# Final mLSTM states of a hybrid decoder step: keys as the stationary operand, states turned back later, stored from the used queries' place

## The reference, cut to what matters

```python
w_state = jnp.exp(b[..., -1:] - b + ig - m_new[..., None])
C_new = decay[..., None, None] * C + jnp.einsum('bhs,bhsv,bhsd->bhvd', w_state, v, k)
n_new = decay[..., None] * n + jnp.einsum('bhs,bhsd->bhd', w_state, k)
```

## Time and profile before

| | |
|---|---|
| runs of the kernel before | 676.42, 676.91, 678.39 us (median 676.91) |
| profiled execution, its own time | 678.53 us |
| its span in the trace | 676.8 us |
| PE busy | 645.1 us, 95% of the span |
| DVE, ACT, POOL busy | 48%, 23%, 31% |
| mean granted clock of TensorE | 0.989 |

### The profile page before, as it was taken

How to read it: one execution, slowest core, us unless ns; L and a number is a source line. 1 busy time by engine, 2 the same in 40 slices (tenths; PEclk the granted TensorE clock), 3 DMA queues, 4 the chain that set the end, 5 groups by cost and what they waited for, 6 DMA issues and landing times.

```text
span 676.8 us, 8651 instructions
## 1 busy us (share of the span) xinstructions
PE 645.1 (95%) x3276; PEld 395.5 (58%) x3276; DVE 323.7 (48%) x756; ACT 156.6 (23%) x345; POOL 208.6 (31%) x245
## 2 busy tenths in 40 slices
PE   6999899999999999999999999999999999999982
PEld 3445588887788764446896784444574454333330
DVE  0283447227555973745000875355872424244445
ACT  1113401102542220002111740222324111121144
POOL 4240001002567555513000885012244332111231
PEclk9999999999999999999999999999989999999997
DMA  8994405303363154067940787454449999999598
GB/s 296 390 316 162 140 1 186 125 1 127 96 209 115 62 206 140 16 183 225 384 179 16 240 307 288 185 213 186 181 160 362 413 412 403 376 347 411 205 203 170
DMA packets 45811, 146.14 MB, mean 216 GB/s; under 512 B 5738, under 2 KB 6058, under 8 KB 41663
## 3 DMA queue, kind: packets, MB, share of 16 engines
q1 hardware_dynamic: 31559, 107.50, 42.5%
q0 software_dynamic: 12032, 33.29, 17.3%
q10 hardware_dynamic: 2176, 4.76, 1.8%
HBM read 130.34 MB, written 20.33 MB: 223 GB/s over the span
## 4 chain that ended last, share of the span: by engine, by line
PE 87%; DMA 5%; DVE 3%; ACT 2%; issue 1%; POOL 0%; DVEq 0%; ACTq 0%; POOLq 0%
PE ps L463 17%; PE ps L740 13%; PE ps L1073 12%; PE ps L497 8%; PE ps L576 7%; PE ps L1093 5%; PE ps L578 4%; DMA xn<-y_d 3%; PE ps L836 2%; PE ps L765 2%; PE ps L960 2%; PE ps L649 2%; PE ps L1054 1%; PE ps L664 1%; PE ps L820 1%; PE ps L525 1%
## 5 line engine op out<-in xcount | busy, mean ns | idle before, releaser
L463 PE MATMUL ps<-xT,wring 128*128 128x208 f32 (+1 forms) x512 | 113.7, 383 | 0.3 <-ACT xT L1351 0.3
L463 PEld LDWEIGHTS ps<-xT,wring 128*128 128x128 f32 x512 | 93.2, 190 | 19.0 <-issue 0.4
L740 PE MATMUL ps<-wring,P 128*128 128x512 f32 x224 | 99.2, 596 | 0.0
L740 PEld LDWEIGHTS ps<-wring,P 128*128 128x128 f32 x224 | 41.6, 190 | 49.1 <-issue 49.0
L1073 PE MATMUL ps<-wring,P 128*32 128x512 f32 (+1 forms) x288 | 65.3, 600 | 0.9 <-DVE P L2304 0.9
L497 PE MATMUL ps<-wring,P 128*128 128x512 f32 x128 | 57.5, 607 | 1.0 <-DVE P L1714 0.8
L2465 POOL TENSOR_SCALAR rstd<-agg 128x1 f32<-128x1 f32 (+1 forms) x15 | 16.8, 1121 | 112.1 <-DVE agg L1699 112.0
L2304 DVE COPY P<-ps 128x512 f32<-128x512 f32 x11 | 7.6, 692 | 76.4 <-PE ps L1054 71.0
L1073 PEld LDWEIGHTS ps<-wring,P 128*32 128x32 f32 (+1 forms) x288 | 22.2, 130 | 36.2 <-issue 36.2
L497 PEld LDWEIGHTS ps<-wring,P 128*128 128x128 f32 x128 | 24.5, 195 | 30.7 <-issue 30.5
L2607 POOL TENSOR_TENSOR P<-P,xT 128x2048 f32<-128x2048 f32 x8 | 36.0, 4528 | 20.9 <-DMA xT<-sq_d 19.0
(11 more groups left out here) (444 smaller groups left out, 1090.0 us busy)
## 6 DMA issues: line engine op xcount, KB each, us to landing
wring<-in_w_in SPq DMA_DIRECT2D x5, 2048.0 KB, 8.6
wring<-in_w_gate SPq DMA_DIRECT2D x10, 1024.0 KB
wring<-in_w_up SPq DMA_DIRECT2D x10, 1024.0 KB
P<-in_w_down SPq DMA_DIRECT2D x10, 1024.0 KB, 11.1
P<-in_cache_mem_k SPq DMA_DIRECT2D x8, 1024.0 KB, 6.7
P<-in_cache_mem_v SPq DMA_DIRECT2D x8, 1024.0 KB, 5.4
y_d<-P POOLq DMA_DIRECT2D x1, 4160.0 KB, 27.4
wring<-in_ca_wv SPq DMA_DIRECT2D x2, 2048.0 KB, 20.8
```

The costliest lines, as they stand in the source:

```text
L463: last = mm(out, lhs(k), rhs(k), start=(k == 0), stop=(k == n - 1))
L740: last = mm(bk[:, :], src[:, k, START[t]:START[t] + TR], w[:, k, :], start=(k == 0), stop=(k == KC - 1))
```

## The change

The state is now made the other way round: a tile's weighted keys are held and the values with their column of ones move (129 columns). One accumulation of four matmuls gives C transposed (key x value) in 128 columns and n as the 129th column. DVE copies both to the place of the head's queries, `stateT` and `state_n` in `qT`. Later PE turns `stateT` back through the identity into a bank of the DVE ring (`transpose_state`), and DVE copies it to `stateC` in the same place (`take_turned_state`). POOL stores C from there, and n from a column of 128 partitions. For heads 0 to 2 the turn stands behind the turn of the same head's output; for head 3 it stands between L771 and `rows_project(1)`, and its copy behind `residual(0)`. `state_out` moves in POOL's queue: behind the masks for heads 0 and 1, behind `load_state(6)` for head 2, behind `norm_rstd(0)` for head 3. The norm's vectors no longer wait for the states' stores but for the last state's matmuls. SP waits for all stores before the cross-attention caches are loaded over the queries' place.

```diff
-        Cout = gb[:, 1, 0:512].rearrange("p (b k) -> p b k", b=2)
+        stateT, stateC, state_n = qT[:, :, 0:HD], qT[:, :, HD:2 * HD], qT[:, :, 2 * HD:2 * HD + 1]
...
                 bk = bank_d()
                 for i in range(NQT):
-                    mm(bk[:, 0:HD], vn[:, i, h, 0:HD], kw[:, i, :], start=(i == 0), stop=(i == NQT - 1))
-                for i in range(NQT):
-                    last = mm(bk[0:1, HD:2 * HD], vn[:, i, h, HD:HD + 1], kw[:, i, :], start=(i == 0), stop=(i == NQT - 1))
+                    last = mm(bk[:, 0:HD + 1], kw[:, i, :], vn[:, i, h, :], start=(i == 0), stop=(i == NQT - 1))
                 last.then_inc(dve_full, 1)
                 at["state", h] = nd[0]
+
+            def transpose_state(h):
+                pe.wait_ge(dve_free, at["state", h])
+                nc.tensor.transpose(bank_d()[:, 0:HD], stateT[:, h, :], ident).then_inc(dve_full, 1)
+                at["turned state", h] = nd[0]
...
             transpose_heads(0)
+            transpose_state(0)
             numerators(1)
...
             transpose_last(1)
+            transpose_state(1)
             numerators(2)
...
             transpose_last(0)
+            transpose_state(2)
             numerators(3)
...
                 mm(bk[0:TR, :], mixT[:, KC - 1, 0:TR], w[:, KC - 1, :], start=False, stop=True).then_inc(dve_full, 1)
+            transpose_state(3)
             rows_project(1, WO, mixT)
...
             sp.wait_ge(act_full, at["pool"])
+            for i in range(2):
+                sp.wait_ge(c_out[i], 64)
             for n in range(3):
                 kv_load(n)
...
             def take_state(h):
                 bk = full()
-                if h >= 2:
-                    dve.wait_ge(c_out[h % 2], 32)
-                V.tensor_copy(Cout[:, h % 2, 0:HD], bk[:, 0:HD])
-                V.tensor_copy(Cout[0:1, h % 2, HD:2 * HD], bk[0:1, HD:2 * HD]).then_inc(dve_free, 1)
+                V.tensor_copy(stateT[:, h, :], bk[:, 0:HD])
+                V.tensor_copy(state_n[:, h, :], bk[:, HD:HD + 1]).then_inc(dve_free, 1)
+
+            def take_turned_state(h):
+                bk = full()
+                V.tensor_copy(stateC[:, h, :], bk[:, 0:HD]).then_inc(dve_free, 1)
...
             take_heads(0)
+            take_turned_state(0)
             head_norm1(1)
...
             take_heads(2)
             take_last(0)
+            take_turned_state(2)
             pool_diff(1)
...
             dve.wait_ge(gb_in, 32)
             residual(0, x1_ready)
+            take_turned_state(3)
             carried(7)
...
             def state_out(h):
-                pool.wait_ge(dve_free, at["state", h])
-                pool.dma_start(o_pC[0, 0, h], Cout[:, h % 2, 0:HD]).then_inc(c_out[h % 2], 16)
-                pool.dma_start(o_pn[0, 0, h:h + 1], Cout[0:1, h % 2, HD:2 * HD]).then_inc(c_out[h % 2], 16)
+                pool.wait_ge(dve_free, at["turned state", h])
+                pool.dma_start(o_pC[0, 0, h], stateC[:, h, :]).then_inc(c_out[h % 2], 16)
+                pool.dma_start(o_pn[0, 0, h].rearrange("(k one) -> k one", one=1), state_n[:, h, :]).then_inc(c_out[h % 2], 16)
...
                 load_state(2 * h + 2)
                 load_state(2 * h + 3)
-                state_out(h)
                 head_rstd(h + 1, TR, NQT)
                 masks(h + 2)
-            state_out(2)
+                state_out(h)
             update_state(4)
             update_state(5)
             window_sums()
             load_state(6)
+            state_out(2)
             head_rstd(3, TR, NQT)
-            state_out(3)
             update_state(6)
...
-            for i in range(2):
-                pool.wait_ge(c_out[i], 64)
+            pool.wait_ge(dve_full, at["state", 3])
             norm_vectors("ln1_g", "ln1_b")
...
             norm_rstd(0)
+            state_out(3)
             update_state(7)
```

More of the change, by code:

```diff
@@ L1965, in _ @@
             take_last(1)
+            take_turned_state(1)
             head_norm1(2)
```

## The result

The changed kernel took 682.41 us (median of 5 runs, 679.79 to 682.62) beside 677.12 us for the kernel before in the same rounds (5 runs, 676.42 to 678.39): a ratio of 1.0071, 95% interval 1.0056 to 1.0085, so 3.8 to 5.8 us slower. The forecast was 681.2, range 679.4 to 683.8. The profiled execution took 682.43 us, its span is 680.6.

The account below looks back on a forecast made before the run. PE, busy 95%, was taken as the bound, but its savings before tile 1 were swallowed by one wait for a bank: 676.91 + 4.25, about 681.2 us, range 679.4 to 683.8.

Parts of the forecast that it names:

- Work saved on PE: State matmuls of four heads: 1.05 us saved each, 0.11 added each by the turn, 3.76 us less work in all.
- Heads 0 to 2 give nothing: Score blocks after the state: PE waits 1.05 us longer for DVE's copy; together between -0.4 and +0.3, taken as 0.
- the two bounds: DVE's second state copy, shrunk to 128x1: between 0 and 0.20 us saved a head, taken as 0.10.
- `wo0` not earlier: After head 3's state: the last pooling matmuls need DVE's pooling difference, so PE reaches `wo0` at about 248.0.
- The ring: Head 3's turn takes tile 1's first bank; tile 1 gets `wo0`'s, emptied by L1997; 6.95 us spent of 3.3 slack.
- The landing of `gb`: Norm's vectors in POOL's queue: `state_out(2)` adds 1.2 us of issues, 0.4 passed on, so they land at 265.5.
- What costs nothing: Moved stores and SP's new wait: last store issued about 272.5, SP waits only after 304, 30 us of cover.
- the clock: Rival (a): PE's pause before tile 1 lowers the clock, 1.9 us more, perhaps twice that, 683.1 to 685; chance 0.13.
- 4.25: Start of tile 1's row projection (L740): 266.3 against 262.06, 4.25 us later, after PE stands 4.0 us; the shift stays.

Follow-up runs that it names:

- experiment 4: Kernel before with only the cheap state: keys held, values moving, n stored as a column, turn back left out; 676.21 us, ratio 0.9985.
- (1): Changed kernel with head 3's turn moved behind tile 1's output projection, its copy and store moved along; 677.04 us, ratio 0.9995 to the kernel before.
- (2): Changed kernel with the loads of the norm's vectors moved in front of `update_state(6)`; 677.99 us, ratio 1.0009 to the kernel before.
- (3): Kernel before plus one needless turn of the identity in the place of head 3's turn, copied behind `residual(0)`; 681.77 us, ratio 1.0066.
- experiment 8: Changed kernel with head 3's turn behind tile 1, norm's vectors before `update_state(6)`, DVE's products before its head norms; 680.19 us, ratio 1.0022 to the kernel before.
- experiment 5: Changed kernel repeated on a second chip: 684.27 us, 1.0082; with four needless matmuls filling PE's pause: 682.22 us, 1.0052 (ratios to the kernel before).
- experiment 7: Kernel before with only DVE's order changed: `take_state(h)` and `products(h+1)` before `head_norm1(h)` for heads 0 to 2; 679.61 us, ratio 1.0029.

## Why the prediction was right, point by point

- **Work saved on PE**: 1.05 us forecast per state, 1.06 read (1.95 - 0.89); the turn 0.11 forecast, 0.10 read. Right.
- **Heads 0 to 2 give nothing**: 66.33 us after, 66.36 before; shown by the brackets at L649, and by experiment 4, where the state is cheap and nothing else is changed. Right, and the second copy saved 0.13 to 0.14, between the two bounds.
- **`wo0` not earlier**: 248.0 forecast, 247.95 read, with 0.91 us of waiting for the pooling difference in front.
- **The ring**: forecast as the step that decides. Shown three times, once from each side: take the turn out of its place and the loss is gone (1), let the bank come free earlier and it is gone (2), add a bank to the kernel before and it is there (3).
- **The landing of `gb`**: 265.5 forecast, 265.38 read. The chain in front of and behind it too: root 251.3 and 251.39, norm 252.7 and 252.79, samples' product 253.85 and 253.82, tile 1 266.3 and 266.22.
- **What costs nothing**: the stores of n as a column took 6.8 to 8.2 us from issue to landing, 1.7 to 6.7 as a row. The last was issued at 273.00 and so was down by about 281, where 304 was allowed.
- **Mis-sized: the clock.** The forecast wrote that the clock fell 5.2 us after the last work at the end of the kernel, that the pause here is shorter, and gave the fall 0.13. It fell in all four profiled executions with a pause of 2.60 us or more in front of tile 1 (2.60, 3.64, 3.76, 4.06), and in neither of those with 0.49 us or with the pause filled down to 1.63. Counted from the last work in front of the pause it fell after 2.2 us once and after 4.5 to 5.0 us three times, those three times with PE already back at work, so being shorter than 5.2 us did not protect the pause. One row at the end of the kernel, where PE simply stopped, was no bound for a pause in the middle of it. The size given for it, 1.9, was about right: tile 1 took 1.8 us more in three of the four and 1.55 in the fourth. The sum with it is 4.25 + 1.8 = 6.05, and the runs show 3.8 to 5.8. The forecast's 4.25 lies in the interval too, near its lower end, but that is in part luck: it leaves out a term of 1.8 that the trace shows. The rule of the Trainium skill that was set beside this step ("TensorE: Matmul & The Clock Gate", section "HAM oscillation — how this bites in real kernels"), by which waits between bursts send the engine back to half rate, agrees with these four traces; the two with the shorter pauses show no fall.
- **Left open**: why the measured difference comes 0.2 to 2.2 us short of 6.05. In the profiled pair it is the wait in the routing (0.9 by the shift) and the fall at the experts' start (1.5), but both come and go between executions of one kernel, and the record does not show how often each kernel has them.

## What to carry to other kernels

- In a ring of PSUM banks every new use shifts all later ones. Before a small operation is put in, name the bank that the next large block will get, who empties it and what that engine is waiting for then. Here 0.11 us of work cost 5 us in one place and nothing one block later.
- Work taken off the busiest engine is worth something only where no bracket stands behind it. Read in each stage which wait ends last, and what the next one is: with DVE's order changed, a store two engines away took the place.
- A pause of the matmul engine in the middle of a kernel is charged with the slow stretch behind it as well, here 1.8 us on top of 3.8.

## What was not expected of the hardware

- In front of tile 1 the granted clock fell with each of the pauses of 2.60 to 4.06 us, once before PE was back (2.2 us after its last work), otherwise 0.7 to 1.3 us after it had resumed, and it stayed at 1.2 GHz for 3.4 us. In experiment 8 it fell with a pause of 1.94 us, for 3.4 us, and with one of 4.44 us, for 6.8. With 1.63 us in front of tile 1 (experiment 5) and 1.32 us in front of the pooling matmuls (experiment 7) it stayed up.
- At the experts' start it fell while PE was counted busy for 3.00 of 3.00 us (in the windows shown), for 6.8 us in two executions, 3.4 to 3.5 in six and not at all in five.
- The second of the two vector loads landed 5.6 us after its issue in one place of the queue and 8.8 in another.
